# Fewer mLSTM units inside the sample attention, and stride-16 exponentials fed by a GpSimd subtraction

## The reference, cut to what matters

```python
# prompt attention, for each of the patterns (128, 1), (512, 4), (2048, 16)
s = einsum(qb, kc) * scale + bias ; mx = max(s) ; p = exp(s - mx)
o = einsum(p, vc) / sum(p)          # patterns are later weighed by their softmax denominators
# sample attention: the same over a cache of 1024 rows and the new rows
# mLSTM: short causal convolution of width 4 and SiLU on the q and k inputs, then per head
s = einsum(q, k) * exp(dlog - mt) ; num = s @ v + e_inter * (C @ q) ; den = ...
```

## Time and profile before

| | |
|---|---|
| median of the runs | 2525.51 us |
| the profiled execution's own time | 2526.61 us |
| its span, first to last instruction | 2524.8 us |
| mean granted TensorE clock | 0.990 |
| prompt attention, the last stride-16 units of the last pair | 391.3 to 409.8 us of the span |
| sample attention, TensorE's first to last instruction | 413.0 to 516.3 us |
| first matmul of the mLSTM stage | 520.46 us |

### The profile page before, as it was taken

How to read it: one execution, slowest core, us unless ns; L and a number is a source line. 1 busy time by engine, 2 the same in 40 slices (tenths; PEclk the granted TensorE clock), 3 DMA queues, 4 the chain that set the end, 5 groups by cost and what they waited for, 6 DMA issues and landing times.

```text
span 2524.8 us, 45764 instructions
## 1 busy us (share of the span) xinstructions
PE 2429.8 (96%) x16691; PEld 1402.8 (56%) x16904; DVE 1558.1 (62%) x3694; ACT 1118.2 (44%) x2667; POOL 324.2 (13%) x699
## 2 busy tenths in 40 slices
PE   6999998989999999899999999999999999999998
PEld 4557775567859586645544444444444444444444
DVE  6757886556767667677798755555655773122323
ACT  5438996544546454533365433333333452111211
POOL 1002221011112121212100112222200000000202
PEclk9999999999999999999999999999999999999999
DMA  6431346611111111153333443444422445444655
GB/s 226 138 108 51 106 116 177 196 45 36 36 53 38 50 37 62 63 182 132 117 101 97 121 138 122 132 136 129 144 82 72 117 134 186 164 143 151 178 165 119
DMA packets 275779, 290.16 MB, mean 115 GB/s; under 512 B 15853, under 2 KB 236078, under 8 KB 274150
## 3 DMA queue, kind: packets, MB, share of 16 engines
q1 hardware_dynamic: 265334, 253.42, 32.3%
q0 software_dynamic: 10224, 33.82, 5.0%
HBM read 192.21 MB, written 94.97 MB: 114 GB/s over the span
## 4 chain that ended last, share of the span: by engine, by line
PE 53%; DVE 3%; issue 1%; ACT 1%; DMA 0%; POOL 0%; DVEq 0%; POOLq 0%; ACTq 0%
PE f_bank L3155 8%; PE f_bank L3156 7%; PE f_bank L3154 7%; PE f_bank L121 4%; PE f_bank L120 4%; PE f_bank L119 4%; PE f_banks_then_turned L3155 2%; PE f_banks_then_turned L3154 2%; PE f_banks_then_turned L3156 2%; PE f_bank_gate L120 1%; PE f_bank_gate L121 1%; PE f_bank_gate L119 1%; PE f_bank_up L119 1%; PE f_bank_up L120 1%; PE f_bank_up L121 1%; PE o_ps_y L119 1%
## 5 line engine op out<-in xcount | busy, mean ns | idle before, releaser
L119 PE MATMUL m_ps_then_y<-keys_then_head_then_ffn,act 128*128 128x256 bf16 x640 | 175.6, 274 | 0.3 <-ACT z_then_patterns L1048 0.3
L120 PE MATMUL m_ps_then_y<-keys_then_head_then_ffn,act 128*128 128x256 bf16 x640 | 175.5, 274 | 0.0
L121 PE MATMUL m_ps_then_y<-keys_then_head_then_ffn,act 128*128 128x256 bf16 x640 | 175.5, 274 | 0.0
L3156 PE MATMUL f_bank<-act,keys_then_head_then_ffn 128*128 128x512 bf16 x395 | 149.7, 379 | 0.9
L3154 PE MATMUL f_bank<-act,keys_then_head_then_ffn 128*128 128x512 bf16 x384 | 145.5, 379 | 0.9 <-DVE z_then_patterns L3600 0.6
L3155 PE MATMUL f_bank<-act,keys_then_head_then_ffn 128*128 128x512 bf16 x382 | 144.8, 379 | 0.8
L3498 DVE TENSOR_TENSOR keys_then_head_then_ffn<-keys_then_head_then_ffn 128x512 bf16<-128x512 f32 x150 | 100.4, 686 | 45.2 <-ACT keys_then_head_then_ffn L3278 44.4
L3155 PE MATMUL f_bank<-mix_m_lo_then_tokens,keys_then_head_then_ffn 128*128 128x512 bf16 x320 | 121.3, 379 | 1.1 <-issue 0.2
L3156 PE MATMUL f_bank<-mix_m_hi_then_tokens,keys_then_head_then_ffn 128*128 128x512 bf16 x320 | 121.3, 379 | 0.0
L1098 DVE SCALAR_TENSOR_TENSOR keys_then_head_then_ffn<-z_then_patterns,m_hd,keys_then_head_then_ffn 128x512 f32<-128x512 f32 x99 | 74.4, 751 | 70.3 <-ACT keys_then_head_then_ffn L1051 68.0
L693 ACT ACTIVATE a_probs<-a_probs,a_low 128x256 f32<-128x256 f32 (+1 forms) x288 | 115.1, 466 | 5.4 <-DVE a_low L876 4.5
(11 more groups left out here) (749 smaller groups left out, 7015.8 us busy)
## 6 DMA issues: line engine op xcount, KB each, us to landing
m_w_raw<-in_w_gate SPq DMA_DIRECT2D x30, 512.0 KB, 3.9
keys_then_head_then_ffn<-in_w_up SPq DMA_DIRECT2D x30, 512.0 KB, 4.0
f_t_then_hidden<-hidden_blocks SPq DMA_DIRECT2D x18, 704.0 KB, 5.5
keys_then_head_then_ffn<-hidden_blocks SPq DMA_DIRECT2D x18, 704.0 KB, 5.4
hidden_blocks<-keys_then_head_then_ffn SPq DMA_DIRECT2D x44, 256.0 KB, 2.9
hidden_blocks<-mix_m_hi_then_tokens SPq DMA_DIRECT2D x44, 256.0 KB, 2.6
hidden_blocks<-mix_m_lo_then_tokens SPq DMA_DIRECT2D x44, 256.0 KB, 2.8
act<-in_w_down POOLq DMA_DIRECT2D x22, 512.0 KB, 5.5
```

Of the source, the lines that this page charges most:

```text
L119: pe.matmul(out, w_hi, x_hi, start=first, stop=False, skip_group_check=in_parts)
L120: pe.matmul(out, w_hi, x_lo, start=False, stop=False, skip_group_check=in_parts)
L121: return pe.matmul(out, w_lo, x_hi, start=False, stop=last, skip_group_check=in_parts)
L3156: mm = nc.tensor.matmul(bank[:, :], low, t_hi[q][j][:, kt, :], start=False, stop=kt == HK - 1, skip_group_check=True)
```

## The change

It has two parts.

In the **prompt attention**, units of stride 16 get a new step on GpSimd, `lower_scores`: once VectorE has made a unit's minima, GpSimd subtracts them from the 128x512 scores in place, the minimum spread over the 128 columns of its tile. ScalarE waits for that (`lowered`) and then takes one exponential of 128x512 without a bias in place of four of 128x128. GpSimd does this four units ahead and before `keep_low`, and its sorting of queries is spread over every second of the first sixteen steps of a pair.

In the **sample attention**, `FIRST_UNITS` is 4. Units 0, 1 and 2 are done in batches 1, 3 and 5, unit 3 after the last transposes, and units 4 to 7 at the start of the mLSTM stage. Tanh, convolution and SiLU follow: ScalarE's tanh and VectorE's convolution of units 0, 1, 2 are in batches 2, 4, 6, the SiLU of 0 and 1 in batches 3 and 5. The second and third weight are loaded in batches 3 and 5 and split in 6 and 7; the fourth is loaded in the mLSTM stage, behind the row `u`, and split there at i = 4.

```diff
--- before.py
+++ after.py
@@ -212,6 +212,8 @@
     LAST_CHUNK_UNIT = next(u for u in range(per_pair) if units[u][3][-1][1] * P >= CHUNKS[NC - 2][0])
     PT, PROBS, STAGES, AHEAD, TURNED, LOWS, SORTS = 3, 3, 5, 4, 3, 8, 8
     stores_before = lambda slot, step: (step - slot + STAGES - 1) // STAGES
+    ready_made = lambda pair, pat, a, q_tiles: pat == 2
+    lowered_by = lambda u: sum(ready_made(*unit) for unit in units[0:u + 1])
 
     with ExitStack() as ctx:
         sb = lambda n, s, d=F32, to=ctx: to.enter_context(nc.sbuf_tensor(n, s, d))
@@ -270,10 +272,10 @@
         bias_in = sems.new("a_bias_in0", "a_bias_in1")
         store = sems.new(*(f"a_store{i}" for i in range(STAGES)))
         (w_hi_done, w_split, zeroed, q_ready, q_hi_done, q_done, rows_ready, rows_kept, vh_done, v_done,
-         gates_turned, k_ready, k_kept, k_high, k_done, s_ready, s_done, exp_done, p_turned, p_high, p_done, pv_done, o_kept, q_sorted, low_kept) = sems.new(
+         gates_turned, k_ready, k_kept, k_high, k_done, s_ready, s_done, exp_done, p_turned, p_high, p_done, pv_done, o_kept, q_sorted, low_kept, lowered) = sems.new(
             "a_w_hi_done", "a_w_split", "a_zeroed", "a_q_ready", "a_q_hi_done", "a_q_done", "a_rows_ready",
             "a_rows_kept", "a_vh_done", "a_v_done", "a_gates_turned", "a_k_ready", "a_k_kept", "a_k_high", "a_k_done", "a_s_ready",
-            "a_s_done", "a_exp_done", "a_p_turned", "a_p_high", "a_p_done", "a_pv_done", "a_o_kept", "a_q_sorted", "a_low_kept")
+            "a_s_done", "a_exp_done", "a_p_turned", "a_p_high", "a_p_done", "a_pv_done", "a_o_kept", "a_q_sorted", "a_low_kept", "a_lowered")
 
         def q_pieces(i):
 
@@ -447,6 +449,15 @@
                     pool.wait_ge(s_done, u + 1)
                     nc.gpsimd.tensor_copy(stage[step % STAGES][:, 0:n, a, HD_A + 1], low[:, u % LOWS, 0:n]).then_inc(low_kept, 1)
 
+                def lower_scores(u):
+                    pair, pat, a, q_tiles = units[u]
+                    if not ready_made(*units[u]):
+                        return
+                    here = probs[u % PROBS][:, :].rearrange("p (j c) -> p j c", j=len(q_tiles))
+                    least = low[:, u % LOWS, 0:len(q_tiles)].unsqueeze(2).to_broadcast([P, len(q_tiles), CHUNK // len(q_tiles)])
+                    pool.wait_ge(s_done, u + 1)
+                    nc.gpsimd.tensor_tensor(here, here, least, ALU.subtract).then_inc(lowered, 1)
+
                 def inverse_rms(t):
                     s, n = t % X_SLOTS, rows_of(t)
                     pool.wait_ge(ss_ready, t + 1)
@@ -460,11 +471,15 @@
                 pool.wait_ge(power_ready, 1)
                 for t in range(n_rows):
                     inverse_rms(t)
+                for u in range(AHEAD):
+                    lower_scores(u)
                 for u in range(n_units):
+                    if u + AHEAD < n_units:
+                        lower_scores(u + AHEAD)
                     keep_low(u)
                     pair, at = u // per_pair, u % per_pair
-                    if at < SORTS:
-                        sort_queries(pair, at)
+                    if at % 2 == 0 and at < 2 * SORTS:
+                        sort_queries(pair, at // 2)
 
             @block.tensor
             def _(pe):
@@ -685,6 +700,10 @@
 
                 def exponentials(u):
                     pair, pat, a, q_tiles = units[u]
+                    if ready_made(*units[u]):
+                        act.wait_ge(lowered, lowered_by(u))
+                        nc.scalar.activation(probs[u % PROBS][:, :], probs[u % PROBS][:, :], ACT.Exp, scale=-1.0).then_inc(exp_done, 1)
+                        return
                     act.wait_ge(s_done, u + 1)
                     at = 0
                     for j, (r, b) in enumerate(q_tiles):
@@ -956,7 +975,7 @@
         engine.wait_ge(sem, value)
 
 
-FIRST_UNITS = 8
+FIRST_UNITS = 4
 
 
 class HeadUnits:
@@ -1180,8 +1199,9 @@
         ps_tok = [ps_big[0][:, q * GATE_SEGS:(q + 1) * GATE_SEGS] for q in range(TAB_SIZE)]
         ps_tok_s = ps_big[0][0:NSAMP, TAB_SIZE * GATE_SEGS:TAB_SIZE * GATE_SEGS + P]
         ps_decay, ps_decay_s = ps_big[1][:, 0:GATE_SEGS], ps_big[1][:, GATE_SEGS:GATE_SEGS + H_M * DEC_BATCH]
-        W_LOADS = {2: 1, 3: 2, 5: 3}
-        W_SPLITS = {3: 1, 5: 2, 7: 3}
+        UNIT_AT = {1: 0, 3: 1, 5: 2}
+        W_LOADS = {3: 1, 5: 2}
+        W_SPLITS = {6: 1, 7: 2}
 
         def own_tokens(mix_a, rows, pair, b0, b1):
 
@@ -1356,7 +1376,8 @@
                         turn_tokens()
                         turn_s_tokens()
                         spread_decays()
-                    units.unit(pe, 0, b)
+                    if b in UNIT_AT:
+                        units.unit(pe, 0, UNIT_AT[b])
                     hold(o_kept, b)
                     if 1 <= b <= O_FIRST:
                         turn_rows(b - 1, 1 - slot)
@@ -1396,6 +1417,7 @@
                     turn_k(1, 1, 0, pair)
                 batches(attend)
                 turn_rows(DEC_BATCH - 1, (DEC_BATCH - 1) % 2)
+                units.unit(pe, 0, FIRST_UNITS - 1)
 
             @block.scalar
             def _(act):
@@ -1442,15 +1464,16 @@
                 def attend(b, slot, nth, more):
                     if more:
                         exponential(b + 1, 1 - slot)
-                    if b:
-                        units.tanh_unit(act, 0, b - 1)
+                    if b - 1 in UNIT_AT:
+                        units.tanh_unit(act, 0, UNIT_AT[b - 1])
                     act.wait_ge(p_turned, b + 1)
                     new = CACHE_TILES * Q_TILES
                     nc.scalar.activation(p_t[slot][:, 0:new], ps_p[:, 0:new], ACT.Copy)
                     nc.scalar.activation(p_t[slot][0:DEC_SEQ, new:], ps_new, ACT.Copy).then_inc(p_kept, 1)
                     if more == 2:
                         keep_k(b + 2, slot, [0])
-                    units.keep_unit(act, 0, b)
+                    if b in UNIT_AT:
+                        units.keep_unit(act, 0, UNIT_AT[b])
                     if more == 2:
                         keep_k(b + 2, slot, range(1, PAIRS))
                     if b in W_SPLITS:
@@ -1482,6 +1505,7 @@
                 batches(attend)
 
                 keep_outputs(1)
+                units.keep_unit(act, 0, FIRST_UNITS - 1)
 
             @block.vector
             def _(dve):
@@ -1635,12 +1659,12 @@
                         keep_ends()
                     if b == 2:
                         keep_columns()
-                    if b:
-                        units.convolve(dve, 0, b - 1)
+                    if b - 1 in UNIT_AT:
+                        units.convolve(dve, 0, UNIT_AT[b - 1])
                     if more:
                         normalise(b + 1, 1 - slot)
-                    if b >= 2:
-                        units.silu(dve, 0, b - 2)
+                    if b in (3, 5):
+                        units.silu(dve, 0, UNIT_AT[b] - 1)
                     if b == 0:
                         running_sum()
                         running_maximum()
@@ -1788,7 +1812,7 @@
                     sp.dma_start(u[:, :], g.u_dram[h:h + 1, :].to_broadcast([P, SEQ])).then_inc(u_in, 16)
                     if h:
                         units.weights(sp, h, 2)
-                        units.weights(sp, h, 3)
+                    units.weights(sp, h, 3)
                     after(sp, exp_done_s, h)
                     sp.dma_start(u_s[:, :], g.u_sample_dram[h:h + 1, :].to_broadcast([NSAMP, NSAMP])).then_inc(us_in, 16)
                     after(sp, c_store, h * 16)
```

## The result

| | before | after |
|---|---|---|
| median | 2528.08 us (6 runs) | 2541.5 us (6 runs) |
| ratio, 95% interval | | 1.0053 (1.0041 to 1.0066) |
| profiled execution's span | 2524.8 us | 2539.5 us |
| mean granted clock | 0.990 | 0.988 |

The change costs 13.4 us, 10.4 to 16.7 by the interval. The two profiled spans lie 14.7 us apart. The forecast was 2541 us, which was +15.9 us on a median of 2525.51 us; two of its terms were wrong and made up for each other, and the kernel before now has a median 2.6 us higher.

The account below looks back on a forecast made before the run. TensorE, busy for 96% of the span, was taken as the bound, with ScalarE full in the last stride-16 units. 2526.6 + 3.3 (prompt) + 12.6 (sample) = 2542.5 us profiled, 2541 against the median; range 2536 to 2547, wider 2530 to 2549.

Parts of the forecast that it names:

- GpSimd's loop: Prompt attention, stride-16 units: GpSimd's subtraction lies on a loop of 4.24 us for two units; last pair +2.3 us.
- The first two pairs: Prompt attention, first two pairs: three rounds of the loop and 0.8 us at entry, +0.5 us each.
- Rival (a): Prompt attention: GpSimd's step is hidden and ScalarE's relief counts, total 2531 us; decides below 0.99 us; chance 0.12.
- The moved units: Start of the mLSTM stage: units 5 to 7 and 0.7 us for unit 4 move there, +16.2 us.
- Rival (d): mLSTM stage: the moved units fill its gaps, first a wait of 2.96 us, total 2538 us; chance 0.05.
- What the batches give back: Sample attention: batches that lose a unit or get a smaller one give back 3.6 us in all.
- Batch 0: Sample attention: value products start earlier without a unit, less a 1.1 us wait for key tiles; gain 2.2 us.
- rival (c): Worse gaps: clock falls in batch 0 and stays low (+3), subtraction takes 1.5 us (+3), total 2547 us; chance 0.15.
- Batch 2: Sample attention: runs like batch 4, 11.6 us against 11.72 for a step with a unit; gain 0.1 us.
- Batch 4: Sample attention: stays as it is, since unit 4's 0.7 us lay before the same wait; gain 0.
- Batch 6 to the end: Sample attention: batch 6's products start 2.8 us earlier, less 1.5 for the clock, gain 1.3 us; batch 7 and end even.
- Rival (b): Sample attention: the clock stays up in batches 2, 4 and 6, giving back 4.4 us, total 2537 us; chance 0.15.

Follow-up runs that it names:

- e6: Kernel before with the prompt attention's part alone, GpSimd's subtraction left out and the wide exponential waiting for VectorE: ratio 0.9956 to the kernel before.
- e7: Kernel before with the prompt attention's part alone, plus a second GpSimd instruction (product by 1.0) behind each subtraction: ratio 1.0099 to the kernel before.
- e3: Kernel after with ScalarE's tanh moved behind the copy of the turned probabilities in batches 2, 4 and 6: ratio 1.0027 to the kernel before.
- e9: Kernel after with 12 useless matmuls (half a unit) added in each of batches 2, 4 and 6: ratio 1.0046 to the kernel before.
- e2: Kernel before with the sample attention's part of the change alone: ratio 1.0052 to the kernel before, +13.1 us.

## Why the prediction was right

The time (2541 forecast, 2541.5 measured), the sign and the range came out. That the times agree to half a us is luck: the step was forecast at +15.9 us and measured at +13.4, on a median of the kernel before that stands 2.6 us higher. Of the signs that the prediction named, the 2.1 us between exponentials (measured 13.07 / 7 = 1.87) and the 1.2 to 1.4 us of GpSimd's line (1.04) did not come, the 16 us at the start of mLSTM did. By its steps:

**GpSimd's loop: right in kind, too dear.** The round forecast at 4.24 us for two units is there, with each exponential behind POOL, at 3.83 (401.77 - 397.94). Three terms were too large: minimum to exponential took 401.24 - 400.08 = 1.16 us and not 1.42, as the subtraction took 1.04 and not 1.28; the exponential held the copy back by 0.53 and not 0.63; high copy to low copy took 398.55 - 397.94 = 0.61 and not 0.66. Together 0.41. The two hand-overs within the 1.16 are 0.12 us together, forecast 0.14; the rows that the prediction named for 0.07 each show 402.40 - 402.37 = 0.03, and its 1.16 - 3 x 0.18 gives 0.62 and not 0.63. The Trainium skill (GPSIMD Engine Reference, section 3.1) gives 2.6 cycles an element, from which the prediction estimated 1.1 us; the 1.04 of the trace stands nearer to that estimate than to the row of 1.28 that I took. The last pair's seven units took 13.07 us, four of 1.58 and three of 2.26, as long as before, and the last pair costs +0.4 and not +2.3.

**The first two pairs: -0.7 each and not +0.5.** The entry cost 1.1 us (forecast 0.8), the units gave 1.2 (forecast 0.25, with the dear round), and the last exponential, 0.6 us shorter, was counted in the last pair alone. So the prompt part measured -1.0 us (interval -3.8 to +1.8) and not +3.3. What also was not in the sum is the end of the stage, where SyncE's stores keep 1.3 us. Rival (a), a hidden GpSimd, is refuted all the same: e6 and e7 show the step on the path. Its decision point was right: 1.16 us is over the 0.99.

**The moved units: right.** From the first mLSTM matmul to the first rows it takes 544.18 - 520.04 = 24.14 us, before 528.10 - 520.46 = 7.64: +16.5, forecast 16.2. Rival (d) fails: the first wait moved with unit 8.

**What the batches give back: right in the rule, wrong in three of its terms.** Forecast 3.6 us, measured -0.4 (95.28 against 94.84 us from the second scores to the mLSTM stage).
- Batch 0: 2.2 forecast, 0.1 measured. The products did begin early, at 430.10, and the wait for VectorE's key tiles came as foreseen, 0.97 us. But the clock fell twice (0.70 over the batch), which only rival (c) held. The first fall, from 425.3 us on, lies ahead of both waits. In e3 and e9, with one fall, the same batch gave back 1.7 and 2.0 us, so the 2.2 forecast were nearly there.
- Batch 2: 0.1 forecast, 0.16 measured, by the mechanism given.
- Batch 4: 0 forecast, -0.97 measured. That unit 4's 0.7 us in front of the wait are worth nothing was wrong in these two executions: the wait grew from 2.76 to 3.44 us, and 6.8 us at half clock follow now, 3.4 before.
- Batch 6 to the end: 1.3 forecast, 0.26 measured. The products start at +6.31, as forecast, but 5.1 us of lowered clock follow and not 1.7.

So rival (c)'s first half came true in this execution, at +4.0 us over all batches, and its second, the dearer subtraction, did the opposite. Rival (b) is refuted: the clock fell in every such batch, here and in e2. What decides whether and for how long it falls stays open. In the first mLSTM chunks 3.4 us of lowered clock stand before and 1.7 after, which gave back 1.4 us that the sum did not have.

Added up, in the profiled executions: prompt -2.3 (1.1 of it the chance at 199 us), from there to the second scores +1.4 (the stores and a longer first step), batches +0.4, moved units +16.5, first chunks -1.4; together 14.7 us. Two errors of some 4 us, GpSimd too dear and the gaps too cheap, hid each other, and that too is luck.

## What to carry to other kernels

Before filler work is taken out of a stage that waits for other engines, price a gap as the gap and the lowered clock behind it, and rather thin the filler out over all gaps than leave it whole in half of them: halves cost nothing here where whole units in every second batch cost 13 us. A helper engine's step is priced by the round that it lies on; before making the step faster, look for the instruction in another stream that closes the round too early: moving it was worth 6 us over the prompt part alone, and 3 us without that step. And when a local gain doesn't reach the end, sum the lowered clock by stage first.
